# One small fp32 product in six stages, another order in Mamba's row step, and some buffers 32 bytes further on

## What is computed

```python
STAGES = ["ffn", "mamba", "ffn", "ffn", "moba", "ffn", "sb", "cffn", "dsa", "cffn"]   # the kernel's list

def modulate(x, g, c_act, w, b):
    m = c_act @ w + b
    shift, scale, gate = jnp.split(m, 3, axis=-1)
    h = rmsnorm(x, g) * (1.0 + scale[:, None, :]) + shift[:, None, :]
    return h, gate[:, None, :]

def swiglu(h, w_gate, w_up, w_down):                    # ffn: 1024 -> 2816 -> 1024
    return (jax.nn.silu(h @ w_gate) * (h @ w_up)) @ w_down

def mamba2_mixer(h, w_in, ...):                         # mamba
    proj = h @ w_in                                     # z, x, B, C and dt
    ...                                                 # causal convolution of width 4, silu
    decay = jnp.exp(jnp.where(causal, acum[:, :, None] - acum[:, None, :], -jnp.inf))
    w = cb[..., None] * decay * dt_k[:, None]
    y_intra = jnp.einsum('btsgr,bsgrp->btgrp', w, x_k)
    ...
    return rmsnorm(y * jax.nn.silu(z), norm_w) @ w_out
```

## Time and profile before

| | us |
|---|---|
| runs | 1877.92, 1882.82, 1885.87 |
| median | 1882.82 |
| profiled execution | 1880.71 |
| its span, first to last instruction | 1878.9 |
| PE busy in it | 1780.6 |
| DVE busy | 1445.2 |
| ACT busy | 961.7 |
| mean granted clock of PE | 0.99 |

### The profile page before, as it was taken

The page is one execution under the profiler, slowest core; times in us unless marked ns, Lnnn a source line. Parts: engine busy times, 40 slices in busy tenths (PEclk is TensorE's granted clock), DMA queues, the critical chain, the costliest instruction groups (busy, mean ns, idle before and its releaser), DMA issues.

```text
span 1878.9 us, 34059 instructions
## 1 busy us (share of the span) xinstructions
PE 1780.6 (95%) x14600; PEld 1720.5 (92%) x14600; DVE 1445.2 (77%) x1718; ACT 961.7 (51%) x1256; POOL 0.2 (0%) x4
## 2 busy tenths in 40 slices
PE   2998999999999999999989999998998999999999
PEld 2998989998999999999979999898898988879999
DVE  7799988877789879986557897655799767557666
ACT  3343466666534453345665344555644555665553
POOL 0000000000000000000000000000000000000000
PEclk9999999999999999999999999999999999999999
DMA  9997834343499859984435997333394545324551
GB/s 399 406 381 310 337 114 157 137 173 140 175 378 362 318 222 356 360 322 147 157 113 221 370 363 296 113 149 121 128 341 182 199 144 181 125 91 175 183 183 41
DMA packets 67278, 426.11 MB, mean 227 GB/s; under 512 B 7264, under 2 KB 10352, under 8 KB 30448
## 3 DMA queue, kind: packets, MB, share of 16 engines
q1 hardware_dynamic: 63216, 415.21, 58.1%
q10 hardware_dynamic: 3968, 9.63, 1.5%
HBM read 423.74 MB, written 3.17 MB: 227 GB/s over the span
## 4 chain that ended last, share of the span: by engine, by line
PE 84%; DVE 10%; ACT 3%; issue 2%; DMA 1%; SPq 0%; DVEq 0%; ACTq 0%
PE bank L1371 24%; PE bank L1373 24%; PE bank L1372 24%; DVE w_lo L817 3%; PE bank L1431 2%; DVE macc L848 1%; DMA modws<-mods 1%; PE bank L1701 1%; PE bank L1384 1%; PE bank L1386 1%; DVE mix L1003 1%; PE bank L1391 1%; PE bank L1543 1%; PE bank L1682 1%; DVE mix L828 1%
## 5 line engine op out<-in xcount | busy, mean ns | idle before, releaser
L1371 PE MATMUL bank<-h_hi,w_hi 128*128 128x256 f32 x2864 | 806.6, 282 | 13.8 <-DVE w_lo L817 13.1
L1372 PE MATMUL bank<-h_lo,w_hi 128*128 128x256 f32 x2864 | 800.6, 280 | 0.0
L1373 PE MATMUL bank<-h_hi,w_lo 128*128 128x256 f32 x2864 | 800.5, 280 | 0.0
L817 DVE TENSOR_TENSOR w_lo<-raw,w_hi 128x2048 fp32r<-128x2048 f32 x277 | 633.0, 2286 | 127.2 <-ACT w_hi L421 126.7
L421 ACT ACTIVATE w_hi<-raw 128x2048 fp32r<-128x2048 f32 x277 | 529.4, 1911 | 151.2 <-PE bank L1373 142.7
L1371 PEld LDWEIGHTS bank<-h_hi,w_hi 128*128 128x128 f32 x2864 | 542.3, 189 | 18.7 <-DVE w_lo L817 14.9
L1372 PEld LDWEIGHTS bank<-h_lo,w_hi 128*128 128x128 f32 x2864 | 542.5, 189 | 0.1
L1373 PEld LDWEIGHTS bank<-h_hi,w_lo 128*128 128x128 f32 x2864 | 541.3, 189 | 0.0
L1371 PE MATMUL bank<-a_hi,w_hi 128*128 128x256 f32 x1280 | 362.2, 283 | 0.0
L1372 PE MATMUL bank<-a_lo,w_hi 128*128 128x256 f32 x1280 | 359.4, 281 | 0.0
L1373 PE MATMUL bank<-a_hi,w_lo 128*128 128x256 f32 x1280 | 359.2, 281 | 0.0
(11 more groups left out here) (256 smaller groups left out, 1654.7 us busy)
## 6 DMA issues: line engine op xcount, KB each, us to landing
raw<-weights SPq DMA_DIRECT2D x277, 1024.0 KB, 5.1
modws<-mods SPq DMA_DIRECT2D x144, 768.0 KB, 6.4
mix<-mods SPq DMA_DIRECT2D x6, 1024.0 KB, 8.3
mix<-mods ACTq DMA_DIRECT2D x8, 512.0 KB, 9.2
modws<-mods SPq DMA_DIRECT2D x2, 1024.0 KB, 12.3
biases<-scratch ACTq DMA_DIRECT2D x1, 2048.0 KB, 13.7
mix<-biases ACTq DMA_DIRECT2D x4, 512.0 KB, 3.9
par<-params ACTq DMA_DIRECT2D x1, 1189.0 KB, 8.5
```

Of the source, the lines that this page charges most:

```text
L817: eng.tensor_tensor(w_lo[g % NW][:, :], raw[g % NRAW][:, :], w_hi[g % NW][:, :], ALU.subtract).then_inc(sems["wlo"], 1)
L1371: eng.matmul(dst, ah, bh, start=start, stop=False, skip_group_check=skip)
L1372: eng.matmul(dst, ah, bl, start=False, stop=False, skip_group_check=skip)
L1373: return eng.matmul(dst, al, bh, start=False, stop=stop, skip_group_check=skip)
```

## The change

Three edits. In `ffn` of the PE program (for ffn and cffn stages alike) one plain fp32 product, 128 columns of ones by the first 96 columns of `tri`, is written to bank 6 between gate 0 and up 0. Its result is used nowhere; bank 6 is next written by the sums of squares of the next stage, which start afresh. In `rows` the bf16 product comes first and opens the accumulation, and the fp32r product closes it and gives the signal. And `small` has 12 columns instead of 4, which moves each buffer behind it by 32 bytes: `a_hi` from byte 198176 of a partition to 198208, `a_lo` from 200224 to 200256, `mix` from 202272 to 202304, `acg` from 196640 to 196672, `sel` from 194592 to 194624. `h_hi` stays at 109120.

```diff
@@ build
-        small = sb("small", [P, 4])
+        small = sb("small", [P, 12])
@@ block.tensor, ffn
                 gate(0, 0, 0, True)
+                eng.matmul(bank[6][:, 0:96], con_("ones"), con_("tri")[:, 0:96], start=True, stop=True)
                 up(0, 0, 1, True)
@@ block.tensor, mamba, rows
                     b = bank[6 + h % 2]
-                    eng.matmul(b[:, 0:384], sel[:, h * P:(h + 1) * P], acg, start=True, stop=False,
+                    diag = b[:, :].rearrange("p (a b c) -> p a b c", a=2, b=2)[:, :, 0, :]
+                    eng.matmul(diag, ident_b, below_b.unsqueeze(1).to_broadcast([P, 2, P]), start=True, stop=False,
                                skip_group_check=True)
-                    diag = b[:, :].rearrange("p (a b c) -> p a b c", a=2, b=2)[:, :, 0, :]
-                    k.inc("br", eng.matmul(diag, ident_b, below_b.unsqueeze(1).to_broadcast([P, 2, P]),
-                                           start=False, stop=True, skip_group_check=True))
+                    k.inc("br", eng.matmul(b[:, 0:384], sel[:, h * P:(h + 1) * P], acg, start=False, stop=True,
+                                           skip_group_check=True))
```

## The result

The changed kernel took 1859.52 us (median of 4 runs, 1857.99 to 1862.69), the kernel before on the same chip 1881.96 (4 runs, 1877.92 to 1885.87). The ratio is 0.988, with a 95% interval of 0.986 to 0.991: faster by 22.4 us, where 28 had been predicted. The profiled execution took 1857.99 us with a span of 1856.2 and a mean granted clock of 0.99, as before.

A forecast was written before the change was run, and what follows sets the result against it. PE bounds the kernel: matmul count times start-to-start pace. Gains 20.4 + 1.7 + 0.7 + 2.3 + 2.2 + 1.0 = 28.3 us off 1880.7 give 1852.4; with 2.1 for the median, 1854, range 1844 to 1874.

The forecast's parts named there:

- puts PE into the quick pace, whatever it had: Small product before the up blocks: always brings 113.3 ns per matmul, gaining 4.5 us in a slow stage, costing 0.25.
- Rule F: Rival theory of the follow-ups: the small product turns the pace over, quick to slow and slow to quick; no chance given.
- Stages 3, 5 and 9: FFN stages called slow throughout: each gains 4.5 from the product, 2.5 on down blocks, less 0.25; together 20.4 us.
- rival (a): FFN stages: a wait near the fold or in the first block turns some slow again; 6.7 us lost each; chance 0.17.
- some 3 us: Tight place at the fold in stages 3 and 5: PE may restart slow, costing at most this for the stage's rest.
- Stage 0: 4.5 us, not 2.3: Doubtful first FFN stage: 1.8 us from the product plus 0.8 on down blocks, less 0.25; 2.3 us gain predicted.
- The term that was halved for want of a row: Stage 0, blocks before the fold's wait: quickening worth 3.6 us, half taken, 1.8, since PE idles between product and block.
- The shift: Down blocks over a_hi and a_lo: a multiple of 64 saves 4.0 ns per matmul when quick, 0.7 when slow.
- Rival (b): Down blocks: something other than the 32-byte offset slows a_hi, so they stay at 117.3 ns; 12.7 us lost, 1867; chance 0.06.
- Mamba's row step: New order of the row products in Mamba: price 0 to 0.9 us, 0.5 taken; Mamba as a whole gains 2.2 us.
- The pace term: Mamba's 13 slow blocks behind the row steps: turning quick gains 0 to 2.8 us; half, 1.4, taken.
- Attention: Attention stages' 12 blocks that stream a_hi: the shift gains 2.3 us at 4.0 ns, 0.4 at 0.7 ns; 1.0 taken.

The follow-up runs named there:

- e1: The kernel before with the small fp32 product in front of the first up block alone; 1870.96 us, ratio 0.995.
- e6: The changed kernel with the small product also in front of the up blocks in the loop, 60 products more; 1882.09 us.
- e8: The changed kernel with DVE's fold of the modulation in two halves, behind the gate and the up block's split; 1853.36 us, ratio to before 0.987.
- e10: The changed kernel again, unaltered, measured beside e11 and e12 on the same chip; 1859.36 us, ratio to before 0.988.
- e11: The changed kernel with the fold in two halves, the same as e8, measured once more; 1851.96 us, ratio to before 0.985.
- e12: The changed kernel with the fold in three pieces: transposes behind the gate block's split, one reduction behind up's, one behind down's; 1853.42 us, ratio to before 0.986.
- e2: The kernel before with the 32-byte shift of the buffers alone (small with 12 columns); 1877.30 us, ratio 0.997.
- e3: The kernel before with the other product order in Mamba's row step alone; 1879.96 us, ratio 0.999.
- e4: The changed kernel without the small product, so the shift and the row order only; 1877.04 us, ratio 0.998 to the kernel before.
- e9: The changed kernel with the small product one block later, behind the first up block instead of in front; 1860.31 us in one execution.
- e5: The changed kernel with two small products in a row in front of each first up block; 1864.11 us in one execution.
- e7: The changed kernel with h_hi and h_lo moved 32 bytes past a multiple of 64, a_hi and a_lo left on one; 1891.15 us.

## Why the prediction was right, and where it was not

**The product in front of the up blocks: right for its place, wrong as a law.** All six FFN stages of the kernel after are quick behind it. Over the seven kernels that have one product there and h on a multiple of 64 (after, e1, e6, e8, e10, e11, e12) the up block is quick in 42 cases of 42. Where no product stands there, it is slow in 14 of 14 cases behind a slow gate block, and behind a quick one quick in 5 and slow in 6 (stages 2 to 9 of before, e2, e3, e4, e9). Stage 0 stands apart: of the five kernels without a product there four (e2, e3, e4, e9) had a quick first up block too, so its seven cases say little. A look at the first gate blocks would have been worth having beforehand: in stages 5 and 9 of before, called slow from end to end, they were quick, and the pace changed at the first up block. The step that failed is "puts PE into the quick pace, whatever it had", which the prediction drew from the ends of five stages. e6 and e9 show 55 products in unbroken streams, and behind each of the 28 that met the quick pace PE was slow. The evidence of the earlier trace rows was taken behind a down block at 117.3 ns, so over the misplaced `a_hi`, and the shift took just that away: in stages 2 and 5 of before, 2, 3 and 5 of e1 and 2 and 3 of e3, all with such a down block in front, the last block was quick. So the prediction had the right result at the chosen place for a reason that doesn't hold, and in that it was lucky. The same place in the kernel after, timeline of PE at the end of stage 2:

```profile
653.06 0.28 PE L1373 MATMUL bank<-a_hi,w_lo 128*128 128x256 f32 x1
653.17 0.35 PE L1423 MATMUL bank<-folded,con 128*128 128x96 f32 x2
653.31 0.36 PE L1371 MATMUL bank<-h_hi,w_hi 128*128 128x256 f32 x1
```

In front of L1423 a step is 0.11 us, and the block behind it now goes at 118. It costs 0.2 us and no more, since the stage ends there. Rule F does not cover all stage ends either. With the shift in, an unbroken quick stream met L1423 in 19 cases (stages 2, 3 and 5 of after, e5, e8 to e12). At the ends of stages 2 and 5 it turned slow, 13 of 13; at the end of stage 3 the quick pace went on, 6 of 6 (e5, e8 to e12; in e10 30 matmuls from 841.78 to 845.18, 113.3 ns). What is different in stage 3 is not known.

Why the chosen place works although the product turns the pace: the first gate block is never both quick and unbroken when it ends. Timeline of PE in the kernel after, the end of the first gate block in stage 2, then in stage 3:

```profile
482.32 2.09 PE L1391 MATMUL bank<-h_lo,w_hi 128*128 128x256 f32 x16
484.24 0.36 PE L1468 MATMUL bank<-con 128*128 128x96 f32 x2
```

```profile
668.64 2.05 PE L1391 MATMUL bank<-h_lo,w_hi 128*128 128x256 f32 x16
670.53 0.36 PE L1468 MATMUL bank<-con 128*128 128x96 f32 x2
```

In stage 3 the gate block is slow: its sixteen L1391 take 1.89 us, 118 ns each without a break, and the product turns slow into quick. In stage 2 it is quick, and sixteen quick steps would be 1.81 us, but 1.92 pass: PE catches up with DVE (the last slice of `h_lo` is ready at 483.84, PE's first matmul on it starts at 483.90), and the sixteenth starts 0.22 us after the fifteenth instead of 0.11. Behind such a hitch and the product PE went on quick in 17 of 17 cases, four of them in stage 0. That a hitch and a product together give quick is counted, not explained; e5 says that the explanation is not simply one turn for each break.

**Stages 3, 5 and 9: 16.3 us of 20.4.** Stages 5 and 9 gave 6.2 and 6.6 against 6.8. Stage 3 gave 3.5, and there a part of rival (a) came true, in the way the prediction named at the earlier trace rows. DVE at the fold of stage 3 in the kernel after, then PE:

```profile
746.89 3.44 DVE L828 STREAM_TRANSPOSE mix<-macc 128x1536 f32<-128x1536 f32 x2
750.25 3.37 DVE L831 TENSOR_REDUCE folded<-mix 128x48 f32<-128x1536 f32 x2
...
755.39 2.29 DVE L817 TENSOR_TENSOR w_lo<-raw,w_hi 128x2048 fp32r<-128x2048 f32 x1
```

```profile
757.70 0.28 PE L1373 MATMUL bank<-a_hi,w_lo 128*128 128x256 f32 x1
757.81 0.32 PE L1371 MATMUL bank<-h_hi,w_hi 128*128 128x256 f32 x1
757.96 0.28 PE L1372 MATMUL bank<-h_lo,w_hi 128*128 128x256 f32 x1
```

`w_lo` is ready at 757.68, PE starts the block at 757.81 in step, but its next matmul comes 0.15 us later instead of 0.11, and from there to the last block of the stage the pace is 117.8. So 40 ns cost 3.3 us, against "some 3 us". The wait itself is nothing, as predicted. The other late starts of this kind did no harm: in stages 2 and 5 of the kernel after, 2, 3 and 5 of e9 and e10, and 3 and 5 of e5 the margin at the fold was 0.13 to 0.14 us too, the next matmul came after 0.141 to 0.145 us, and the pace held, ten times. In the case that turned it came after 0.153. Nor do those few ns decide: the last block of stage 9 begins like that in seven of the kernels, after 0.142 to 0.153 us, in the kernel after with the same 0.153 (from 1847.24), and the pace held each time. So one late start in eighteen of this kind turned it, and what decides is open. In e8 the DVE's order at this place is:

```profile
746.41 3.43 DVE L828 STREAM_TRANSPOSE mix<-macc 128x1536 f32<-128x1536 f32 x2
...
751.59 2.29 DVE L817 TENSOR_TENSOR w_lo<-raw,w_hi 128x2048 fp32r<-128x2048 f32 x1
```

There `w_lo` is ready at 753.88 for a block that PE starts at 757.33, with nothing late about it. Stage 3 took 186.0 to 186.2 us in e8, e11 and e12, and in e10 as well.

**Stage 0: 4.5 us, not 2.3.** The term that was halved for want of a row came in whole: 1.9 us passed between product and up block (46.18 to 48.04), and PE was quick behind it. With 3.6 for 1.8 the prediction would have had 4.1. But that is not shown to be the product's doing. Without it stage 0 was quick at the same place in e2, e3, e4 and e9, and took 199.1, 201.5 and 199.1 us in e2, e3 and e4, against 198.5 in the kernel after and 200.6 in e10. The kernel before, with its 203.0, had the worse draw, so most of the 4.5 is luck.

**The shift: right.** Down blocks take 5.44 us in the kernel after, as gate and up blocks, and e7 moved the cost to h. Rival (b) is out: by it the shift does nothing, and with the product in place the shift and the row order together were worth 11.4 us, near the 12.7 that the prediction put on the shift. (In that sum stage 0 stands with 1.8, the whole of its down blocks, where the forecast had counted the doubtful five only by half; 1.3 would fit, and 12.2 in all. It changes nothing.)

**Mamba's row step: its price was mis-sized.** The last part of a pair of row steps and the first matmuls behind it, timeline of PE, kernel after:

```profile
296.36 0.28 PE L1373 MATMUL bank<-h_hi,w_lo 128*128 128x256 f32 x1
296.47 0.28 PE L1545 MATMUL bank<-conb 128*128 128x256 bf16 x1
...
297.27 0.44 PE L1547 MATMUL bank<-acg,sel 64*128 64x384 f32 x1
297.64 0.39 PE L1371 MATMUL bank<-h_hi,w_hi 128*128 128x256 f32 x1
...
298.10 0.28 PE L1371 MATMUL bank<-h_hi,w_hi 128*128 128x256 f32 x1
```

From the last matmul of one block to the fourth of the next 1.74 us pass, whether the block in front is over h or over a. In the kernel before it is 294.65 to 296.30, 1.65 us:

```profile
294.65 0.28 PE L1373 MATMUL bank<-a_hi,w_lo 128*128 128x256 f32 x1
294.86 0.44 PE L1543 MATMUL bank<-acg,sel 64*128 64x384 f32 x1
...
296.30 0.28 PE L1371 MATMUL bank<-h_hi,w_hi 128*128 128x256 f32 x1
```

The new order costs 0.1 us for 13 of the 16 pairs and 0.2 for the first, and saves 0.1 in the last two, which stand together: 1.4 us in all, where the prediction's upper end was 0.9 and its value 0.5. The pace term was mis-sized as well. Of the 13 slow blocks behind the rows 12 turned quick (2.6 us), and the first of all, quick before, turned slow (0.2); the 7 behind the output step, quick before, turned slow too (7 x 48 x 4.5 ns, 1.5). That is 0.9, not 1.4. With 1.3 for the down blocks it makes 0.9 + 1.3 - 1.4 = 0.8, and the part of the stage that holds the groups became 0.7 us shorter (268.5 to 470.8 before, 263.2 to 464.8 after). Its beginning took 0.3 longer, and the other 1.0 of the measured 1.4 is luck with the clock in the stage's last block; PE there in the kernel before, then after:

```profile
470.70:476.00 5.30, 5.30 (x33) 0.65 0.00 0
464.70:470.00 5.30, 5.30 (x42) 0.88 0.00 0
```

Nor was the new order needed to turn the blocks behind the rows. In e2, with the old order and the shift alone, the same 12 are quick and those behind the output step slow just the same (46 starts in the 5 us from 290.9), at no price, and Mamba took 239.4 us against 240.7 in the kernel after. Alone (e3) the order made all 14 blocks behind the rows quick too, and left the others so. So with the shift there, the row order is a loss of about 1.3 us: the pairs' 1.4 is read in every one of them, the stage's time in a single execution of e2.

**Attention: 1.0 predicted, -2.7 found.** This can't be held against the shift. Its term is sound where the pace is quick: the blocks over a in the three stages took 69.6 us before, 67.5 in e2 and 67.6 in e10, 2.1 less, though not in the kernel after (69.8), where several of them were slow and one, the last of stage 4, ran mostly at the lower clock (5.35 us, 4.24 before). The largest piece is the first gate block of stage 6, which took 8.3 us instead of 7.0, under a clock that was lower for longer. PE from the start of that block, kernel before, then after:

```profile
1194.00:1202.00 8.00, 8.00 (x56) 0.79 0.00 0
1176.57:1184.57 8.00, 8.00 (x45) 0.61 0.00 0
```

These two blocks cost 2.4 of the 2.7 us. Without the one in stage 4 the blocks over a took 0.9 us less than before, near the forecast's 1.0; some 1.2 us more are spread over the three stages and were not followed. The stages together took 427.3 us before, 430.0 and 428.3 in the two profiles of the changed kernel, 425.8 in e2 and 431.3 in e4, which has the shift too, so one execution differs from the next by more than the term.

**The sum.** The profiled execution lies 5.6 us above the 1852.4 of the sum: stage 3 is 3.3 of it, attention 3.7, Mamba 0.8, stages 5, 7 and 9 together 1.2; stage 0 and the start gave 2.2 and 1.1 more than predicted. (The rest is rounding.) Most of what is missing from the forecast is the turn in stage 3 and the clock in attention; it would have been off by more without the luck in stage 0.

**What stays open.** What the two paces are, and by what a single product turns one into the other, is not known. The Trainium skill (TensorE: Matmul & The Clock Gate, Back-to-back issue gap) gives 262 cycles for 256 columns at the upper clock, 109.2 ns, as the gap of an isolated matmul; for a stream of weight loads and matmuls it has figures at 128 and 512 columns (81 and 131 ns) and none at 256, and it knows of no second pace. The stream here, with a weight load for each matmul, went at 113.3 or 117.8, never at 109. Nor do the runs tell what two products in a row do, or what decides behind a wait. A version with the product, the shift and the spread fold but the old row order should by the above take some 1.3 us less than e11; it was not tried.

## What to carry to other kernels

Read the pace of a long stream of matmuls from start to start and stage by stage: two stages with the same code, clock and busy share can differ by 4%, and the cause then lies where the pace was last disturbed, not in the stage. A short matmul in the stream can turn the pace, so judge such a nudge at its own place and in each stage by itself, and keep the producers ahead there, since 40 ns late cost the rest of a stage once. Compare the turned stages with kernels that lack the nudge before giving it the credit: stage 0 was quick without it. Put a streamed fp32r operand on a multiple of 64 bytes; it costs a few bytes of padding, and it pays in full only where the stream runs at the quick pace.

## What had not been expected of the hardware

- One fp32 product of 96 columns turned a stream of fp32r matmuls of 256 columns from 113.3 to 117.8 ns per matmul or back, in 49 of 49 unbroken streams in e6 and 6 of 6 in e9, and the pace then held for up to 180 us. It is no law: in six kernels with the shift the same shape at L1423 met the unbroken quick pace at the end of stage 3, and the pace went on.
- A matmul that started 40 ns late (757.96 behind 757.81) was followed by the slow pace; seventeen others that were 28 to 40 ns late, ten of them at the same place of a stage, were not.
- A streamed fp32r operand 32 bytes past a multiple of 64 cost 4.0 ns per matmul at the quick pace and 0.7 or less at the slow one.
- An fp32r product in front of the block costs 0.22 us to its second matmul (297.64 to 297.86), a bf16 product in front 0.20 (295.86 to 296.06), but that block itself begins 0.04 us after the bf16 product and 0.37 after the fp32r one. A pair of row steps took 1.74 us in the one order and 1.65 in the other.
